# An encoder step on one core: the conditioning product moved from TensorE to VectorE, and the halves' order turned in all stages

## The reference, cut to what matters

```
for l in range(DEPTH):                                   # DEPTH = 2, D_MODEL = 1024
    mp = split(silu(c_prompt) @ w_ada[l] + b_ada[l], 9)  # c: one vector of 1024 for each of two groups
    ms = split(silu(c_sample) @ w_ada[l] + b_ada[l], 9)
    # for the 512 prompt rows with mp and the 64 sample rows with ms:
    h += 0.5 * m[2] * rmsnorm(swiglu(rmsnorm(h) * (1 + m[1]) + m[0]))     # FFN "a"
    x  = rmsnorm(h) * (1 + m[4]) + m[3]
    P  = x @ w_in                       # q/k/v of two attentions, gating MLP, 3 x 1024 gate logits
    y  = (sig(gA)*(oA@Wa) + sig(gB)*(oB@Wb) + sig(gC)*(oC@Wc)) @ w_out
    h += m[5] * rmsnorm(y)
    h += 0.5 * m[8] * rmsnorm(swiglu(rmsnorm(h) * (1 + m[7]) + m[6]))     # FFN "b"
```

## Time and profile before

| | |
|---|---|
| median of 3 runs | 2848.84 us |
| the profiled execution's own time | 2847.8 us |
| its span (first to last instruction) | 2846.0 us |
| busy: TensorE, VectorE, ScalarE, GpSimd | 2783.9, 1298.3, 971.0, 111.2 us |
| matmul instructions | 21654 |
| moved by DMA | 319.8 MB, 112 GB/s over the span |

### The profile page before, as it was taken

How to read it: one execution, slowest core, us unless ns; L and a number is a source line. 1 busy time by engine, 2 the same in 40 slices (tenths; PEclk the granted TensorE clock), 3 DMA queues, 4 the chain that set the end, 5 groups by cost and what they waited for, 6 DMA issues and landing times.

```text
span 2846.0 us, 49978 instructions
## 1 busy us (share of the span) xinstructions
PE 2783.9 (98%) x21654; PEld 2628.9 (92%) x21654; DVE 1298.3 (46%) x2533; ACT 971.0 (34%) x1821; POOL 111.2 (4%) x210
## 2 busy tenths in 40 slices
PE   7999999999999999999999999999999999999997
PEld 6999999878999989999999999998889999999997
DVE  3444424655544464443264443256555445544423
ACT  4222324444422452222252222244443225422322
POOL 0000000010000000000000000001100000000000
PEclk9999999999999999999999999999999999999999
DMA  6444532333222234432224444323322222222221
GB/s 245 149 148 149 172 121 93 110 123 98 92 82 82 82 104 149 148 134 88 88 86 152 149 149 165 112 100 116 122 96 68 82 82 75 82 82 82 86 87 66
DMA packets 90186, 319.82 MB, mean 112 GB/s; under 512 B 11360, under 2 KB 14464, under 8 KB 89776
## 3 DMA queue, kind: packets, MB, share of 16 engines
q1 hardware_dynamic: 64048, 222.50, 23.4%
q0 software_dynamic: 25920, 94.14, 9.7%
HBM read 305.70 MB, written 11.55 MB: 111 GB/s over the span
## 4 chain that ended last, share of the span: by engine, by line
PE 85%; DVE 7%; ACT 3%; DVEq 2%; issue 2%; DMA 1%; SPq 0%; ACTq 0%
PE ps L668 77%; PE ps L782 2%; PE ps L1013 2%; PE ps L1059 1%; DVE h L1671 1%; ACT w_hi L1162 1%; DVE x_lo L1678 1%; PE ps L1035 1%; DVEq L1670 1%; DVE z L1669 1%; PE ps L677 1%; DMA w_raw<-in_f 1%; ACT sig L1498 1%; ACT x_hi L1254 1%; DVEq L2017 1%
## 5 line engine op out<-in xcount | busy, mean ns | idle before, releaser
L668 PE MATMUL ps<-x_hi,w_hi 128*128 128x290 f32 (+1 forms) x4256 | 973.8, 304 | 22.7 <-DVE x_lo L1678 13.6
L668 PE MATMUL ps<-x_lo,w_hi 128*128 128x290 f32 (+1 forms) x4256 | 935.4, 295 | 0.0
L668 PE MATMUL ps<-x_hi,w_lo 128*128 128x290 f32 (+1 forms) x4256 | 934.8, 295 | 0.0
L668 PEld LDWEIGHTS ps<-x_hi,w_hi 128*128 128x128 f32 x4256 | 686.7, 189 | 95.1 <-issue 65.3
L668 PEld LDWEIGHTS ps<-x_lo,w_hi 128*128 128x128 f32 x4256 | 701.1, 190 | 0.3
L668 PEld LDWEIGHTS ps<-x_hi,w_lo 128*128 128x128 f32 x4256 | 692.7, 189 | 0.0
L1553 DVE TENSOR_TENSOR w_lo<-w_raw,w_hi 128x1024 fp32r<-128x1024 f32 x386 | 468.8, 1222 | 254.2 <-ACT w_hi L1162 251.9
L1162 ACT CAST w_hi<-w_raw 128x1024 fp32r<-128x1024 f32 x386 | 392.9, 1047 | 77.3 <-DMA w_raw<-in_f 77.3
L668 PE MATMUL ps<-hid_hi,w_hi 128*128 128x288 f32 x1344 | 300.8, 295 | 1.8 <-DVE c_col L1610 1.8
L668 PE MATMUL ps<-hid_hi,w_lo 128*128 128x288 f32 x1344 | 300.7, 295 | 0.0
L668 PE MATMUL ps<-hid_lo,w_hi 128*128 128x288 f32 x1344 | 298.7, 293 | 0.0
(11 more groups left out here) (214 smaller groups left out, 2391.8 us busy)
## 6 DMA issues: line engine op xcount, KB each, us to landing
w_raw<-in_f SPq DMA_DIRECT2D x260, 512.0 KB, 3.5
ada_w<-in_ada POOLq DMA_DIRECT2D x128, 512.0 KB, 5.7
w_raw<-in_gate SPq DMA_DIRECT2D x64, 512.0 KB, 3.5
w_raw<-in_tri SPq DMA_DIRECT2D x42, 512.0 KB, 3.5
ada_first<-in_ada SPq DMA_DIRECT2D x4, 2048.0 KB, 17.7
w_raw<-in_wout SPq DMA_DIRECT2D x16, 512.0 KB, 3.4
decay_s<-f_scratch POOLq DMA_DIRECT2D x16, 272.0 KB, 6.0
decay_p<-f_scratch POOLq DMA_DIRECT2D x8, 512.0 KB, 5.9
```

What stands on the lines that cost most here:

```text
L668: r = mm(ps[:, 2 * out + b, 0:width], w, xx[:, cols(b)], start=first and n == 0, stop=last and n == 2)
```

## The change

All modulations but the first two are computed on VectorE. The weights for it are handed over transposed, so that a unit is 128 output features on the partitions by 512 of the 1024 inputs on the free axis (256 KB); silu(c) of both groups is brought to all 128 partitions (`c_half`, one half of the 1024 inputs at a time, by way of DRAM). For each of the two groups one `tensor_tensor_reduce` multiplies the unit by `c_half` and adds the row sums to the modulation's column in `ada_all`. The product written besides is not used; for the first group it goes to PSUM (bank 5 or 6). The 16 modulations are 256 units and 512 such instructions, in f1 (one unit behind the first split and one behind the last of each step i), in f2 (two or three behind each split) and in the merge (two behind the splits of gates 1 and 2 and two before `msum`, in the steps m = 1, 2, 3, 5, 6, 7, until the 32 units of the stage are used up). GpSimd loads a unit when the one two before it has been used, and `c_half` anew when the half changes, which happens 12 times in all, once in the middle of each merge.

Besides: `split_tile` issues the second of its three products in the order half 1, half 0 in all stages; before it did so only in the stages of 288 columns (`columns`). The shift vectors are put behind x later in `full_tiles`. SP waits for the units of f2a before it loads the mixer's inputs, which share the place of `c_half`. At the start SP loads `c_rows` (8 KB) ahead of x, ScalarE takes its silu, and GpSimd writes it to DRAM, loads it spread over the partitions and loads the first two units; before, GpSimd's first load waited until the first modulations' weights had arrived.

```diff
-ADA_PART = {(0, "a"): (16, 64), (0, "b"): (64, 96), (1, "a"): (96, 144), (1, "b"): (144, 144)}
 ADA_COLS = 256
+ADA_K = D_MODEL // 2
+ADA_STAGES = [((l, ph), [l * N_MOD + m for m in mods]) for l in range(DEPTH)
+              for ph, mods in (("f1a", (2, 4)), ("f2a", (3, 5)), ("gate", (6, 7)),
+                               ("f1b", (8, 10) if l == 0 else (8,)), ("f2b", (9,) if l == 0 else ()))]
+def ada_units():
+    half, units, at = 0, [], {}
+    for stage, mods in ADA_STAGES:
+        at[stage] = len(units)
+        for part in (0, 1) if mods else ():
+            half ^= part
+            units += [(stage, half, m * KD + t) for m in mods for t in range(KD)]
+    at[None] = len(units)
+    return units, at
+ADA_UNITS, ADA_AT = ada_units()
+ADA_ENDS = {stage: min(a for a in ADA_AT.values() if a > ADA_AT[stage]) if mods else ADA_AT[stage]
+            for stage, mods in ADA_STAGES}
...
+def c_changes(u):
+    stage, half, _ = ADA_UNITS[u]
+    return u == 0 or half != ADA_UNITS[u - 1][1] or (u == ADA_AT[stage] and stage[1] == "gate")
...
+F2_UNITS = (2,) * 8 + (0, 3, 3) + (2,) * 5 + (0,) * (KF - 16)
+def f1_units(l, ab, i):
+    half = KD // (2 if (l, ab) == (1, "b") else 1)
+    return int(2 <= i < 2 + half or 4 + half <= i < 4 + 2 * half)
+def gate_units(m):
+    return 2 if m in (1, 2, 3, 5, 6, 7) else 0
...
-                for b in halves[::-1] if cols is columns and n == 1 else halves:
+                for b in halves[::-1] if n == 1 else halves:
...
+            sp.wait_ge(ada_used.sem, ada_used.done(0, ADA_ENDS[l, "f2a"] - 1))
...
-        def ada_work(l, ab, s):
-
-            if s and ada_slot(l, ab, s - 1) and ada_slot(l, ab, s - 1)[-1] % KD == KD - 1:
-                ada_turn_in(ada_slot(l, ab, s - 1)[-1] // KD, ada_turn)
-            for n in ada_slot(l, ab, s):
-                ada_piece(n)
...
+        def ada(l, ph, n):
+            for u in range(modulated[0], min(modulated[0] + n, ADA_ENDS[l, ph])):
+                at = ADA_UNITS[u][2]
+                if c_changes(u):
+                    dve.wait_ge(c_half_in.sem, c_half_in.done(0, c_loads(u) - 1))
+                dve.wait_ge(ada_full[u % 2].sem, ada_full[u % 2].done(0, u // 2))
+                for g in (0, 1):
+                    so_far = ada_all[:, at, g:g + 1]
+                    out = ada_w[:, u % 2, :] if g else ada_out[u % 2]
+                    r = V.tensor_tensor_reduce(out, ada_w[:, u % 2, :], c_half[:, g, :], 1.0, so_far,
+                                               ALU.mult, ALU.add, so_far)
+                r.then_inc(ada_used.sem, 1)
+                modulated[0] += 1
...
                     split_lo()
+                    ada(l, ph, f1_units(l, ab, i))
...
                 for _ in range(f2_chunks_begun(o)):
                     split_lo()
-                if o:
-                    ada_finish(l, ab, F1_SLOTS + o - 1)
+                    ada(l, "f2" + ab, next(units))
...
                     if m or br == 2:
                         split_lo()
+                    if br:
+                        ada(l, "gate", gate_units(m))
                     dve.wait_ge(chunk_done.sem, chunk_done.done(0, chunk(l, "gate", 4 * m + br)))
...
                 split_lo()
+                ada(l, "gate", gate_units(m))
                 if m:
                     dve.wait_ge(prod_hi.sem, prod_hi.done(l, KF + m - 1))
...
+        def c_rows_to_dram():
+            pool.wait_ge(c_rows_made.sem, c_rows_made.done(0, 0))
+            dma(c_scratch, c_rows[:, :], c_rows_out)
+            pool.wait_ge(c_rows_out.sem, c_rows_out.done(0, 0))
+        def ada_loads(l, ph):
+            for u in range(ADA_AT[l, ph], ADA_ENDS[l, ph]):
+                _, half, n = ADA_UNITS[u]
+                cols = slice(half * ADA_K, (half + 1) * ADA_K)
+                if c_changes(u):
+                    if u:
+                        pool.wait_ge(ada_used.sem, ada_used.done(0, u - 1))
+                    dma(c_half[:, :, :], c_scratch[:, cols].partition_broadcast(P), c_half_in)
+                if u > 1:
+                    pool.wait_ge(ada_used.sem, ada_used.done(0, u - 2))
+                dma(ada_w[:, u % 2, :], row_of("ada", n - RING_FROM)[:, cols], ada_full[u % 2])
```

More of the change, by code:

```diff
@@ L76, with c_loads @@
 RING_FROM = 2 * KD
-ADA_PART = {(0, "a"): (16, 64), (0, "b"): (64, 96), (1, "a"): (96, 144), (1, "b"): (144, 144)}
 ADA_COLS = 256
+ADA_K = D_MODEL // 2
[14 more added lines that the diff above has]
+            for stage, mods in ADA_STAGES}
+def c_loads(u):
+    return sum(c_changes(v) for v in range(u + 1))
+def c_changes(u):
+    stage, half, _ = ADA_UNITS[u]
+    return u == 0 or half != ADA_UNITS[u - 1][1] or (u == ADA_AT[stage] and stage[1] == "gate")
+SHIFT_AT = {0: 6, 1: 1, 2: 6}
+F2_UNITS = (2,) * 8 + (0, 3, 3) + (2,) * 5 + (0,) * (KF - 16)
[4 more added lines that the diff above has]
+    return 2 if m in (1, 2, 3, 5, 6, 7) else 0
 def running(counts):
@@ L96, in chunk @@
     return l * CHUNK_N + CHUNK_AT[ph][0] + i
[L100 to L106, removed]
 def f2_tiles(o):
@@ L335, in build_program @@
     ada_at = arena[0]
-    ada_w = sb("ada_w", [P, 2, 4 * ADA_COLS])
+    c_half = sb("c_half", [P, 2, ADA_K])
+    ada_w = sb("ada_w", [P, 2, ADA_K])
     mask = sb("mask", [P, NMASK, P], at=ada_at)
@@ L370, in build_program @@
     ada_first = sb("ada_first", [P, 2 * KD, 4 * ADA_COLS], at=first_at)
-    cond = sb("cond", [P, KD, 2], at=first_at + 2 * KD * 4 * ADA_COLS * 4)
+    start_at = first_at + 2 * KD * 4 * ADA_COLS * 4
+    cond = sb("cond", [P, KD, 2], at=start_at)
+    cond_s = sb("cond_silu", [P, 2 * KD + 30], at=start_at + 64)
+    ada_sum = sb("ada_sum", [P, ADA_COLS], at=start_at + 256)
+    c_rows = sb("c_rows", [2, D_MODEL], at=start_at + 256 + ADA_COLS * 4)
     o_hi = sb("o_hi", [P, KD, TOK], F32R, at=big)
@@ L430, in shifted @@
         return ps[:, 2 * p + 1, HALF:HALF + SH]
-    ada_ps = ps[:, 6, 0:ADA_COLS]
-    ada_turn = ps[:, 7, 0:ADA_COLS]
+    ada_out = [ps[:, bank, 0:ADA_K] for bank in (5, 6)]
     start_ps = ps[:, 5:7, 0:HALF]
@@ L443, in build_program @@
     v_more = ps[0:DEC, 7, 384:384 + P]
+    c_scratch = nc.dram_tensor("c_scratch", (2, D_MODEL), F32, kind="Internal").ap()
     scratch = nc.dram_tensor("f_scratch", (DEPTH, B_HEADS, SEQ + SC), F32, kind="Internal").ap()
@@ L459, in build_program @@
     ada_used = S("ada_used", 0)
+    c_rows_in = S("c_rows_in", 0, step=16)
+    c_rows_made = S("c_rows_made", 0)
+    c_rows_out = S("c_rows_out", 0, step=16)
+    c_half_in = S("c_half_in", 0, step=16)
+    shift_made = S("shift_made", 3)
     ada_copied = S("ada_copied", 0)
@@ L576, in _ @@
         sp.dma_start(cond[:, :, :], ins["cond"]).then_inc(cond_in.sem, 16)
+        sp.dma_start(c_rows[:, :], ins["cond_rows"]).then_inc(c_rows_in.sem, 16)
         sp.dma_start(h[:, :, :], ins["x"]).then_inc(h_in.sem, 16)
@@ L854, in ffn @@
                         r.then_inc(f2_done.sem, 1)
-                ada_work(l, ab, F1_SLOTS + o)
             o = KD - 1
@@ L1273, in full_tiles @@
                 evict(l, j, p)
+                if p == SHIFT_AT[j] and not is_last(l, j):
+                    act.wait_ge(shift_made.sem, shift_made.done(l, j))
+                    high_shift(*following(l, j))
         def boundary(l, j, done):
@@ L1507, in _ @@
         A(cond_s[:, 0:2 * KD], cond[:, :, :].rearrange("p k g -> p (k g)"), ACT.Silu).then_inc(cond_ready.sem, 1)
+        act.wait_ge(c_rows_in.sem, c_rows_in.done(0, 0))
+        A(c_rows[:, :], c_rows[:, :], ACT.Silu).then_inc(c_rows_made.sem, 1)
         act.wait_ge(h_in.sem, h_in.done(0, 0))
@@ L1553, in split_lo, with modulated_all @@
             V.tensor_tensor(w_lo[:, s, :], w_in[:, s, :], w_hi[:, s, :], ALU.subtract).then_inc(lo_ready.sem, 1)
+        modulated = [0]
+        def ada(l, ph, n):
[11 more added lines that the diff above has]
+                modulated[0] += 1
+        def modulated_all(l, ph):
+            assert modulated[0] == ADA_ENDS[l, ph], (l, ph, modulated[0])
         def ffn_up(l, ab):
@@ L1639, in full_tiles @@
                 begin(p)
+                if p == SHIFT_AT[j] and not is_last(l, j):
+                    dve.drain()
+                    dve.sem_inc(shift_made.sem, 1)
                 add_y(l, j, p)
-                if p == 1 and not is_last(l, j):
-                    low_shift(*following(l, j), shift_high.done(l, j))
+            if not is_last(l, j):
+                low_shift(*following(l, j), shift_high.done(l, j))
         def newton(out, est, var, total):
@@ L1737, in ffn_down @@
         def ffn_down(l, ab, j):
+            units = iter(F2_UNITS)
             def begin(o):
@@ L1781, in first_ada @@
             ada_add(m, n, first_turn[m])
[L1783 to L1790, removed]
         def modulation(l, j, g):
@@ L2100, in merge @@
                 V.tensor_tensor(m_lo[:, m, :], msum[:, :], m_hi[:, m, :], ALU.subtract).then_inc(prod_lo.sem, 1)
+            modulated_all(l, "gate")
         V.memset(c_stat[:, :, :], 1.0)
@@ L2230, in stage @@
```

(9 more changed lines are left out.)

23 lines of the change are left out of this document (7 added, 16 removed).

## The result

The kernel after takes 2835.19 us (median of 4 runs, 2831.16 to 2838.28); the kernel before took 2848.97 us beside it (4 runs, 2848.16 to 2849.9). The ratio is 0.995, with a 95% interval of 0.9937 to 0.9962: 13.8 us or 0.5% faster. The forecast was 2820 (2798 to 2845), a gain of 29 us: the sign is right and the time lies in the range, but just under half of the gain came. The profiled execution of after took 2835.7 us with a span of 2834.0, against 2847.8 and 2846.0 before, so the two traces have 12 us between them.

The account below looks back on a forecast made before the run. TensorE, busy 98% of the span, was taken as the bound. The terms -77 - 3 + 36 + 5 + 7 + 3 = -29 us gave 2819 from the profiled 2847.8, forecast as a 2820 us median, range 2798 to 2845.

Parts of the forecast that it names:

- products off TensorE, halves' order: In f1 and f2 TensorE loses the conditioning products, -77 us; turning the halves' order in 1984 tiles, -3 us (-15 to +6).
- ten merge stalls with the half change: Units ahead of `msum` make TensorE stand 3.6 us in ten merge steps, +36 us; the new half at m = 3, +5.
- clock: Merge stalls bring TensorE's clock down: two long ones and three of eight shorter ones, +7 us in all (3 to 15).
- start: GpSimd's first 1 MB joins the opening transfer rush, 2.5 us, and SP's one issue more 0.5: +3 us (0 to 4).
- end of the kernel: After the output's transfers: the prediction has no term for it, entered as 0 us.
- rival 1: The row sum runs at half rate with both float32 operands in SBUF: +42 us, 2891 us, slower; chance 0.13.
- the wait of 0.9 us for `tail_gu`: At the end of an f1a (i = 21), without the pieces' cover, TensorE waits 0.9 us in all for `tail_gu`.
- Rival 2: Loads are late: at 7 us a load, the merge's second and third pairs wait 1.5 us each; +30, 2850 us; chance 0.09.
- The half change: At m = 3 of each merge the third pair waits 2.7 us for the new `c_half`, twice, +5 us.
- three of eight: Of the eight merge stalls of about 3.4 us, three were counted as lowering the clock, besides the two long ones.
- rival 3: The clock falls at every merge stall: +8 us on the sum, 2828 us; chance 0.15.

Follow-up runs that it names:

- fillers: The changed kernel with 20 matmuls more (42 at m = 3) into an unread bank in the five stalled steps of each merge: 2822.98 us.
- late_start: The changed kernel with GpSimd's loads of `c_half` and the first units waiting until the first modulations' weights have arrived, as before: 2831.25 us.
- best: The changed kernel with merge units dealt out more evenly, three behind the merge's end, and `c_rows` loaded behind the first modulations' weights: 2777.58 us.
- third_after: The changed kernel with the third pair of units of each merge step moved from ahead of `msum` to behind `m_lo`: 2788.27 us.
- no_order: The changed kernel with the old order of the halves taken back in: 2840.07 us.
- split_loads: The changed kernel with each 256 KB unit loaded by two GpSimd transfers of 128 KB: 2838.83 us.

## Why the gain was half of the forecast

The forecast's terms against the two profiled executions:

| term | forecast, us | measured, us |
|---|---|---|
| products off TensorE, halves' order | -77 - 3 | -79 |
| ten merge stalls with the half change | +36 + 5 | +42 (steps of `fillers`) |
| clock | +7 | +16 (steps), 12 by medians |
| start | +3 | +4.5 |
| end of the kernel | 0 | +4 |
| sum | -29 | -12 |

**What held.** The row sum is at full rate, so rival 1 falls. The Trainium skill (Vector Engine (DVE) Microarchitecture Reference, section 7) has a scalar-tensor-tensor form with two SBUF sources that aren't bf16 at half throughput; this row sum, with two float32 sources in SBUF and an accumulator, takes 747 ns for 512 elements, so the measurement decides against carrying that sentence over to it. f1 and f2 hide the units; the wait of 0.9 us for `tail_gu` appeared. The place of the stalls, their number and the third as the longest came out. A pair of units took 2.69 us and not the 2.8 I chose, so a stall comes to 3.24 and not 3.6; the low bound of 0.67 us for an instruction was the right choice. That 36 + 5 came out at 42 is in part luck: in the steps of `fillers` ten stalls of 3.24 are 32, the two changes of the half add 8.4 instead of 5, and two steps are longer by 1.6 together.

**Rival 2**, late loads: in the merges VectorE waited for a unit's load four times, 7.5 us in all, of which 3.5 and 2.8 are the half changes; 0.8 and 0.4 are left, where the rival had 1.5 twice in each step. What TensorE waited for was `msum`, behind VectorE's own row sums. It falls.

**The half change** was asked for at 822.18 and its first unit could start at 829.39, 7.2 us later, where I had 6.7. With all that hangs on it, the step of m = 3 was 4.6 us longer than the other stalled ones in `fillers` and 3.8 in the second merge, where I had 2.7.

**The step that failed is the clock, mis-sized.** "I count three of eight": the eight short stalls, 3.0 to 4.0 us, lowered it seven times, and with the two long ones it fell behind nine of ten. The mechanism was right, and so was the price of one, 1.5 us taken from the start of f1a; 16 us over nine falls are 1.8. The sum itself gave the stalls 3.6 us, the length of the one in the earlier trace rows behind which the clock was down, so by its own row each should have been counted; "three of eight" had no row at all. The Trainium skill (TensorE: Matmul & The Clock Gate, Part 1) has the clock at half in an idle array, and the prediction, letting it fall at all ten stalls by that, got 15 us; the trace agrees, with nine falls and 16 us by the steps. This was rival 3, whose 2828 us is 7 below the median: 4 of them are the end, 1.5 the start.

**What was not in the sum** is the end. It was put at no change, as if the span ended with the output's transfers, which is so for no kernel here: GpSimd's DRAIN ends last in before too. Its growth of 3.9 us is shown by the traces; its cause is not. That the time lies in the range all the same does not bear out the sum: the range reached up to 2845 for the sake of late loads, which did not come.

**Not settled:** why f1a still begins 2.2 us later in `late_start` than in before (56.16 against 53.95), of which the first matmul explains 1.5; and why executions of after differ by up to 7 us where those of before differ by 2. In `fillers`, without falls of the clock in the merges, four runs still lay 3.5 us apart, in `best`, where the start is changed too, five within 1.8. The 2 us between the starts of the five traces above may be a part of it.

## What to carry to other kernels

When work moves to an engine with 50% idle time, look at what idles ahead of the one instruction that the bound engine waits for next; here VectorE, 58% busy, hid all but 40 of 512 row sums, and those 40, ahead of `msum` where it has no idle time, cost 47 of the 79 us won (`third_after` against after). Moving that one pair behind the instruction gave it back. Count a stall of TensorE of 3 us at its length plus 1.5 to 2 us of lower clock, until a trace shows otherwise; and where work must stay late, matmuls put into the gap are worth trying.

## What the runs showed of the hardware

TensorE's clock fell to 0.50 behind nine of ten stalls of 3.0 to 6.6 us, and behind 38 of 40 (3.0 to 6.9 us) in the four kernels that have them (after, `no_order`, `late_start`, `split_loads`), and stayed there for some 3 to 7 us; once, at 799 to 801 us, it fell only after TensorE was running again. Behind one stall of 3.1 us, at 890, it did not fall, and no row tells why; with matmuls put into the same ten gaps, so that 0.3 to 2.1 us of each stayed idle, it never fell there. A row sum of two float32 operands in SBUF ran at 747 to 755 ns for 512 elements, and the read of its accumulator lay beside the next one, so that they follow every 0.67 us. The last DRAIN of GpSimd, which ends the kernel, took 3.34, 7.26 and 9.13 us with 206, 347 and 603 transfers issued by it.
